# Two ordinary tiles instead of four ahead of the seven-product tiles of a feed-forward stage

## What is computed

```python
def rmsnorm(x, g):
    xf = x.astype(jnp.float32)
    y = xf * lax.rsqrt(jnp.mean(xf * xf, axis=-1, keepdims=True) + EPS)
    return (y * g.astype(jnp.float32)).astype(x.dtype)

def swiglu(h, wg, wu, wd):
    return (jax.nn.silu(h @ wg) * (h @ wu)) @ wd
...
        h = rmsnorm(x, ffn_norm_g[layer, 0])
        x = x + 0.5 * swiglu(h, ffn_w_gate[layer, 0], ffn_w_up[layer, 0], ffn_w_down[layer, 0])
```

## Time and profile before

| what | us |
|---|---|
| median of three runs | 2056.39 |
| the profiled execution, its own time | 2056.34 |
| its span, first to last instruction | 2054.5 |
| PE busy | 2029.2 |
| DVE busy | 1555.1 |
| ACT busy | 1018.3 |
| POOL busy | 298.7 |

### The profile page before, as it was taken

The page is one execution under the profiler, slowest core; times in us unless marked ns, Lnnn a source line. Parts: engine busy times, 40 slices in busy tenths (PEclk is TensorE's granted clock), DMA queues, the critical chain, the costliest instruction groups (busy, mean ns, idle before and its releaser), DMA issues.

```text
span 2054.5 us, 34513 instructions
## 1 busy us (share of the span) xinstructions
PE 2029.2 (99%) x13775; PEld 1771.9 (86%) x13775; DVE 1555.1 (76%) x2437; ACT 1018.3 (50%) x1597; POOL 298.7 (15%) x287
## 2 busy tenths in 40 slices
PE   8999999999999999999999999999999999999999
PEld 6899999788888788999998899999866688999998
DVE  6877776596778898877776787777679857877775
ACT  5544444453436445544445444444467745444444
POOL 0111110001000001111110111111046500111110
PEclk9999999999999999999999999999999999999999
DMA  5333334332153423333333333333750122333332
GB/s 157 103 106 101 101 103 108 94 86 82 50 146 93 95 74 100 103 108 99 102 94 110 94 95 103 113 93 88 144 101 8 42 62 82 113 103 94 106 90 72
DMA packets 325284, 196.06 MB, mean 95 GB/s; under 512 B 14891, under 2 KB 317110, under 8 KB 325126
## 3 DMA queue, kind: packets, MB, share of 16 engines
q1 hardware_dynamic: 322502, 184.21, 30.9%
q0 software_dynamic: 2624, 9.67, 3.0%
HBM read 191.07 MB, written 2.79 MB: 94 GB/s over the span
## 4 chain that ended last, share of the span: by engine, by line
PE 66%; DVE 4%; POOL 2%; issue 1%; ACT 1%; DVEq 0%; ACTq 0%; POOLq 0%
PE ps L2014 9%; PE ps L2016 9%; PE ps L2015 9%; PE ps L2078 4%; PE ps L2079 4%; PE ps L2080 4%; PE ps L1892 3%; PE ps L1894 3%; PE ps L1893 3%; PE ps L2586 1%; PE ps L2101 1%; PE ps L2099 1%; PE ps L2100 1%; PE ps L2557 1%; POOL index_scores L538 1%
## 5 line engine op out<-in xcount | busy, mean ns | idle before, releaser
L560 ACT ACTIVATE w_hi<-w_raw 128x1024 fp32r<-128x1024 f32 (+1 forms) x351 | 361.9, 1033 | 208.9 <-PE ps L1894 109.9
L1034 DVE TENSOR_TENSOR w_lo<-w_raw,w_hi 128x1024 fp32r<-128x1024 f32 (+1 forms) x351 | 419.9, 1196 | 43.5 <-ACT w_hi L560 43.2
L472 POOL TENSOR_TENSOR sq<-w_raw 128x512 f32<-128x512 f32 x72 | 96.6, 1341 | 1179.5 <-DMA w_raw<-in_ffn_w_up 1137.1
L2016 PE MATMUL ps<-h_hi,w_lo 128*128 128x256 f32 x864 | 244.5, 283 | 0.0
L2014 PE MATMUL ps<-h_hi,w_hi 128*128 128x256 f32 x864 | 244.2, 283 | 0.0
L2078 PE MATMUL ps<-act_hi,w_hi 128*128 128x512 f32 x512 | 200.0, 391 | 0.0
L2079 PE MATMUL ps<-act_lo,w_hi 128*128 128x512 f32 x512 | 200.0, 391 | 0.0
L2080 PE MATMUL ps<-act_hi,w_lo 128*128 128x512 f32 x512 | 199.2, 389 | 0.0
L2014 PEld LDWEIGHTS ps<-h_hi,w_hi 128*128 128x128 f32 x864 | 165.6, 192 | 2.7
L2016 PEld LDWEIGHTS ps<-h_hi,w_lo 128*128 128x128 f32 x864 | 165.6, 192 | 0.0
L614 ACT ACTIVATE silu_gate<-silu_gate 128x256 f32<-128x256 f32 x144 | 59.8, 415 | 212.9 <-DVE silu_gate L1228 209.8
(11 more groups left out here) (409 smaller groups left out, 5208.8 us busy)
## 6 DMA issues: line engine op xcount, KB each, us to landing
w_raw<-in_ffn_w_gate SPq DMA_DIRECT2D x88, 512.0 KB, 3.8
w_raw<-in_ffn_w_up SPq DMA_DIRECT2D x88, 512.0 KB, 3.8
w_raw<-in_ffn_w_down SPq DMA_DIRECT2D x64, 512.0 KB, 3.4
w_raw<-in_hy_w_in SPq DMA_DIRECT2D x44, 512.0 KB, 3.8
w_raw<-in_ffn_w_down SPq DMA_DIRECT2D x32, 384.0 KB, 3.5
w_raw<-in_hy_w_out SPq DMA_DIRECT2D x16, 512.0 KB, 4.0
acum_rows<-acum_scratch POOLq DMA_DIRECT2D x4, 1024.0 KB, 10.2
bias_rows<-line_scratch POOLq DMA_DIRECT2D x8, 512.0 KB, 11.4
```

What stands on the lines that cost most here:

```text
L560: act.activation(w_hi[:, s, 0:width[n]], w_raw[:, s, 0:width[n]], ACT.Copy).then_inc(hi_ready, 1)
L1034: dve.tensor_tensor(w_lo[:, s, 0:width[n]], w_raw[:, s, 0:width[n]], w_hi[:, s, 0:width[n]].bitcast(F32), ALU.subtract).then_inc(lo_ready, 1)
L2016: mm = pe.matmul(dst, wl, rh[:, k, :], start=False, stop=k == 3, skip_group_check=True)
```

## The change

The phases become 2, 4, 4, 4 and 8 tiles, and PLAIN becomes 2. So twenty tiles of a stage are seven-product tiles. Sixteen of them (2 to 17) have a pack behind them: the packs behind tiles 2 to 5 hold 12 matmuls (two tiles' worth), the other twelve 24. Tiles 18 to 21 have none. The eight final down outputs have 24 matmuls each. The openings of ScalarE, VectorE and TensorE are written anew, the product `a` of the first seven-product tile goes to bank 4, which its pack waits for, and the fourth input sum of the stages ffn1 to ffn3 gets a buffer of its own. The number of units, their order in the slots and the number of updates of x per stage stay.

```diff
-PHASES = ((0, 4), (4, 4), (8, 4), (12, 4), (16, 6))
-PLAIN = 4
+PHASES = ((0, 2), (2, 4), (6, 4), (10, 4), (14, 8))
+PLAIN = 2
...
+        s4_hi = at("s4_hi", [P, 4, TOK // 2], 92, F32R)
...
         def gate_unit(st, f):
-            return UB[st] + 2 * f + max(0, min(f, LAST + 4) - 4)
+            return UB[st] + 2 * f + max(0, min(f, LAST + 4) - PLAIN)
...
+        def packed(f):
+            return PLAIN <= f < LAST + 4
+
+        def pack_of(f):
+            f0, nf = PHASES[(f - PLAIN) // 4]
+            return f0, nf, (f - PLAIN) % 4
...
-            for m in range(KT):
-                width[gate_unit(st, FT - 1) + 2 + m] = LAST_N * P
+            for f in range(PLAIN, PLAIN + 4):
+                width[pack_unit(st, f)] = 2 * PHASES[0][1] * P
...
-                    if i == 3:
+                    if i == 3 and q == 0:
                         act.wait_ge(unit_used, n + 2 * PLAIN)
...
                 if st == STAGES[0]:
                     rms_out(st)
+                    produce_hi(n + 4)
                 for k in range(KT):
                     act.activation(s_raw[:, k, :], x[:, k, :], ACT.Copy, scale=gains[:, GAIN[st] + k:GAIN[st] + k + 1]).then_inc(s_hi_ready, 1)
-                produce_hi(n + 4)
+                if st != STAGES[0]:
+                    produce_hi(n + 4)
+                    rms_out(st)
+                    s_high(0)
+                silu(0)
                 if st == STAGES[0]:
-                    silu(0)
-                else:
-                    rms_out(st)
-                s_high(0)
+                    s_high(0)
                 s_high(1)
...
                 produce_hi(n + 5)
+                act_high(0)
+                t_high(PLAIN)
                 s_high(2)
...
                 if st == STAGES[0]:
                     line_out()
...
+                silu(1)
+                keep(PLAIN, 0)
+                s_high(3)
+                produce_hi(n + 6)
+                act_high(1)
+                keep(PLAIN, 1)
+                keep(PLAIN, 2)
+                produce_hi(n + 7)
+                keep(PLAIN, 3)
+                silu_half(PLAIN, 0)
+                t_high(PLAIN + 1)
+                produce_hi(n + 8)
+                for f in range(PLAIN + 1, FT):
                     nxt_unit = gate_unit(st, f) + 2
...
+                    silu_half(f - 1, 1)
                     produce_hi(nxt_unit)
...
+                    if not packed(f - 1):
                         keep(f, 0)
                     act_high(f - 1)
                     if f < FT - 1:
                         t_high(f + 1)
...
+                    if packed(f - 1):
                         keep(f, 0)
                     produce_hi(nxt_unit + 1)
...
+                    if packed(f):
                         produce_hi(nxt_unit + 2)
...
+                    keep(f, 1)
+                    silu_half(f, 0)
                     keep(f, 2)
                     keep(f, 3)
...
                 if st == STAGES[0]:
                     scaled(0)
+                    produce_lo(n + 4)
                 h_sums()
-                produce_lo(n + 4)
+                if st != STAGES[0]:
+                    produce_lo(n + 4)
+                    scaled(0)
                 s_low(0)
...
+                product(0)
                 s_low(1)
...
+                last_weight_sums(PLAIN)
                 produce_lo(n + 5)
+                act_low(0)
+                t_low(PLAIN)
+                scaled(1)
                 s_low(2)
...
+                product(1)
+                s_low(3)
+                last_weight_sums(PLAIN + 1)
+                act_low(1)
+                gate_low(PLAIN)
                 produce_lo(n + 6)
...
                 produce_lo(n + 7)
...
+                up_sums(PLAIN)
+                t_low(PLAIN + 1)
                 produce_lo(n + 8)
...
-                for f in range(PLAIN, FT):
+                for f in range(PLAIN + 1, FT):
...
-                    b, a, c = (ps[:, bank + j, HALF[0]] for bank in (BB, BA, BC))
+                    b, a, c = (ps[:, bank, HALF[0]] for bank in (BB + j, 4 if first else BA + j, BC + j))
...
+                    if f == PLAIN:
+                        pe.wait_ge(gate_low_steps, 2 * kb + 1)
...
-                for f in (2, 3):
-                    pe.wait_ge(gate_scaled, gb + f)
-                    unit(n + 2 * f, 2 * (f % 2), h_hi, h_lo, KT)
-                    pe.wait_ge(up_scaled, fb + f - 1)
-                    unit(n + 2 * f + 1, 2 * (f % 2) + 1, h_hi, h_lo, KT)
```

More of the change, by code:

```diff
@@ L686, in ffn @@
                         t_high(f + 1)
-                    if f != PLAIN and f - 1 != LAST + 4:
+                    if packed(f - 1):
                         keep(f, 0)
                     produce_hi(nxt_unit + 1)
[L690 to L693, removed]
+                    if packed(f):
                         produce_hi(nxt_unit + 2)
-                        keep(f, 1)
-                        silu_half(f, 0)
+                    keep(f, 1)
+                    silu_half(f, 0)
                     keep(f, 2)
@@ L1241, in ffn @@
                     scaled(0)
+                    produce_lo(n + 4)
                 h_sums()
-                produce_lo(n + 4)
+                if st != STAGES[0]:
+                    produce_lo(n + 4)
+                    scaled(0)
                 s_low(0)
-                if st != STAGES[0]:
-                    scaled(0)
+                product(0)
                 s_low(1)
-                product(0)
+                last_weight_sums(PLAIN)
                 produce_lo(n + 5)
+                act_low(0)
+                t_low(PLAIN)
+                scaled(1)
                 s_low(2)
-                act_low(0)
+                product(1)
[3 more added lines that the diff above has]
+                gate_low(PLAIN)
                 produce_lo(n + 6)
-                scaled(1)
-                last_weight_sums(PLAIN)
-                product(1)
                 produce_lo(n + 7)
-                act_low(1)
-                t_low(PLAIN)
+                up_sums(PLAIN)
+                t_low(PLAIN + 1)
                 produce_lo(n + 8)
-                scaled(2)
-                product(2)
-                produce_lo(n + 9)
-                act_low(2)
-                for f in range(PLAIN, FT):
-                    nxt_unit = gate_unit(st, f) + 2
-                    added = 4 <= f - 1 < LAST + 4
-                    if f == PLAIN:
-                        scaled(f - 1)
-                    else:
-                        gate_high(f - 1)
+                for f in range(PLAIN + 1, FT):
+                    nxt_unit = gate_unit(st, f) + 2
+                    gate_high(f - 1)
                     product(f - 1)
@@ L2020, in ffn @@
                 s1, s2, s3 = ((s_hi[:, i, :, :], s_lo[:, k0:k0 + 4, h]) for i, k0, h in ((1, 4, HALF[1]), (0, 0, HALF[0]), (2, 0, HALF[1])))
-                s4 = h_hi[:, 0:4, HALF[1]], s_lo[:, 4:8, HALF[0]]
+                s4 = s4_hi[:, :, :] if q else h_hi[:, 0:4, HALF[1]], s_lo[:, 4:8, HALF[0]]
                 def seven(f):
@@ L2037, in seven @@
                     product(b, gate, 0, *a11, True).then_inc(prod_done, 1)
-                    if first:
-                        pe.wait_ge(gate_scaled, gb + PLAIN + 1)
-                    elif second:
+                    if second:
                         pe.wait_ge(up_scaled, fb + PLAIN)
-                    else:
+                    elif not first:
                         pe.wait_ge(gate_low_steps, 2 * (k - 2) + 1)
@@ L2066, in down_pack @@
                 def down_pack(f):
-                    u, i, f0 = pack_unit(st, f), f % 4, f // 4 * 4 - 4
+                    u, (f0, nf, i) = pack_unit(st, f), pack_of(f)
                     s = u % SLOTS
                     pe.wait_ge(lo_ready, u + 1)
+                    if f == PLAIN:
+                        pe.wait_ge(gate_low_steps, 2 * kb + 1)
                     for j in range(2):
-                        pe.wait_ge(x_upd, XB[st] + 2 * (f - 4) + j - 1)
-                        for k in range(4):
+                        pe.wait_ge(x_upd, XB[st] + 2 * (f - PLAIN) + j - 1)
+                        for k in range(nf):
                             if i == 0:
@@ L2123, in ffn @@
                     seven(f)
-                    if f < LAST + 4:
+                    if packed(f):
                         down_pack(f)
```

49 lines of the change are left out of this document (13 added, 36 removed).

## The result

The changed kernel takes 2118.73 us (median of 4 runs, 2117.48 to 2120.55) against 2056.43 of the kernel before: 1.0304 times as long, 95% interval 1.0292 to 1.0317, or 62 us more. The profiled execution took 2117.66 us with a span of 2115.9. The time lies inside the range given, 14 us above the forecast.

The account below looks back on a forecast made before the run. The prediction took TensorE to bound the kernel: fewer matmuls save 6.8 us, but new waits in openings and ends, less old waits, make +49 in all, so 2056.3 + 49 = 2105 us, range 2080 to 2126.

Parts of the forecast that it names:

- What bounds the kernel: Whole kernel: TensorE, busy 2029.2 of 2054.5 us, sets the span, and every new wait of it lengthens the span.
- What the matmuls give, -6.8: Two ordinary tiles become seven-product tiles, 10.92 to 10.07 us each: 1.7 us a stage, 6.8 over four; down projection costed at nothing.
- The first wait: Third product of tile 2, waiting for VectorE's three `s_low`: 2.2 us in ffn2, 4.5 with mutual blocking; 11.3 in ffn0.
- GpSimd beside VectorE: Stage openings: GpSimd's weight sums and VectorE operations with two SBUF inputs block each other, 1.8 us for tile 2, 0.5 tile 3.
- The upper bound: Openings: every meeting of GpSimd's sums with such VectorE operations, `s_low` included, blocks as in rows 7; total +49 against +31 without.
- The second wait, 5.8: Third product of tile 3, behind tile 4's up unit load, weight sums, `t_high` and `keep`: 5.8 us, 4.1 without blocking.
- Tiles 4 to 6, and 19 and 20: Late `keep` evictions: 2.0 us a stage in tiles 4 to 6; 1.1 us at the fifth product of tiles 19 and 20 each.
- The sum: Whole kernel: +11.3 us each in ffn1 to ffn3, +15 in ffn0, together +49, or +31 without mutual blocking.
- a rival with a chance of 0.15: Clock falls in eight new waits of 4.5 us or more, costing 24 us more: 2129; chance 0.15 for above 2120.
- matmuls more than 0.12 us apart: Sign that would prove the forecast wrong: 256-column matmuls starting further apart than this, which would be the clock.
- Not slower: Rival: the openings keep up, with `s_low(2)` and tile 4's load early enough; 2042, or 2049.5 with old waits; chance 0.10.
- Only the ends wait: Rival: opening keeps up, but tiles 4 to 6 and 19, 20 lose 3 to 4 us a stage; 2050 to 2062; chance 0.07.

Follow-up runs that it names:

- e8: Changed kernel with GpSimd's weight sums of tiles 3 and 4 on 16 of 512 columns, the rest left out: 2102.97 us.
- e6: Changed kernel with unused-result matmuls ahead of the third product of tile 2 only (90 in ffn0, 34 in ffn1 to ffn3): 2118.87 us.
- e3: Changed kernel with ScalarE's keep(f, 1) ahead of the next up unit's high part in tiles whose predecessor has no pack: 2114.12 us.
- e5: Changed kernel with 34 unused-result matmuls per stage ahead of the third product of tile 3 only: 2112.00 us.
- e1: Changed kernel whose first seven-product tile waits for one input low part per product instead of three before the third: 2117.55 us.
- e12: Kernel before with e11's edit, plus ffn0's unit n+4: high part behind ScalarE's third copy, low part ahead of the input sums: 2053.75 us.
- e4: Changed kernel with units n+6 and n+7 split on ScalarE and VectorE ahead of the fourth input sum's split: 2116.64 us.
- e10: Changed kernel with e1, e3, e4, e5 and e9 together: 2105.18 us.
- e7: Changed kernel with VectorE's four input sums on 16 of 256 columns, the rest of that work left out: 2102.37 us.
- e11: Kernel before with keep(f, 1) of each stage's first seven-product tile ahead of the high parts of the next two units: 2054.11 us.
- e9: Changed kernel with ffn0's high part of unit n+4 behind the third of ScalarE's eight copies instead of ahead of them: 2116.81 us.

## Why the prediction was right, and by how much it missed

**What bounds the kernel.** Right: TensorE sets the span, and gaps and slow matmuls between its starts explain 60.4 of the 61.4 us by which it grew.

**What the matmuls give, -6.8.** Right as a count: undisturbed seven-product tiles take 10.07 us, and the final down outputs 43.55 for 192 matmuls, 0.227 each, as costed.

**The first wait.** Right to 0.1 us where its list holds. Moved by the 32.55 us between the two traces (tile 2 at 1178.51 for 1145.96), the forecast has the sums begin at 1166.33 and the third `s_lo` end at 1185.75; measured 1166.26 and 1185.64. (The steps as listed in the forecast add up to 16.9, not 17.1; they are rounded.) In ffn1 it is 5.96: there VectorE makes one low part of 1.22 us between the norm and the sums, so they begin 10.96 us ahead of tile 2, not 12.25, and the wait is longer by about as much. I had taken ffn2 for all three. ffn0 came at 11.24 for 11.3, closer than that wait repeats.

**GpSimd beside VectorE.** The upper bound, which I took, was right: `s_low(0)` and the product cost 0.72 + 1.09 = 1.8 us more, `s_low(2)` 0.5. The rule of the Trainium skill, SBUF — State Buffer, "Who interferes with whom", holds for the meeting that was open: two SBUF inputs on VectorE and a reading GpSimd block each other, and an `s_lo` of 1.21 us becomes 1.76 to 1.94. e8 confirms it: without most of GpSimd's work beside them, `s_lo` and the product take 1.22 and 0.69. What blocking costs in time was not tried by itself, as e8 takes away GpSimd's own time as well.

**The second wait, 5.8.** The chain was right link by link: issue at 1193.05 (forecast 1160.5, or 1193.05 moved), landing after 4.9 for 4.7, sums, `t_high` and `keep` with TensorE at 1204.64 (forecast 1204.45). What failed is the other end, "Tile 2 ends at 1160.5": moved, that is 1193.05, and it ended at 1194.54, as its products behind the first wait ran at 1.2 GHz. TensorE came 1.5 us later and so waited 4.48. e6, which keeps the clock up there, measured 5.6 to 5.9 in all four stages: the forecast's number.

**Tiles 4 to 6, and 19 and 20.** 2.0 a stage became 1.6, and 1.1 became 1.05. In tile 19 the mechanism was right: e3 takes the wait away by the order alone. In tile 20 the order is not all of it, since in e3 a meeting with GpSimd, which the forecast did not have there, keeps 0.86.

**The sum.** It was +49 and came out +62. The term that was mis-sized is the clock: I gave it to a rival with a chance of 0.15 and nothing in the sum. The rival had the fall right at every long wait, and its price wrong: 3 us for each of eight, 24, where slow matmuls make 15.4 and e5 gives back 6.7, all of it behind the second waits. Its counterargument, that work behind a wait is dense here, did not keep the clock. The prediction had named matmuls more than 0.12 us apart as a sign that it was wrong, and on this point it was. The rule of the Trainium skill, TensorE: Matmul & The Clock Gate, "Part 1: The HAM clock gate", that idle time brings the half clock as the default, agrees with all eight, though a wait of 3.02 us in e1 and one of 3.24 in e12 did not bring it. By the table's rows, the first waits are 1.4 us above the forecast, the second waits 5.7 below it, tiles 4 to 6 and 19 and 20 together 2 below, and the slow matmuls 15.4 above. That is +9 of the 12.4 between 49 and the 61.4 of the spans; the rest I have not settled. So the forecast came as close as it did partly by luck: the slow matmuls that it left out also shortened the second waits that it had put in at full length.

**The rivals on the other side.** *Not slower* asked for `s_low(2)` early and an earlier load. e4 sent the load 1.3 us earlier against its stage and gained about 2; e10, with every reordering I had, stays at +49. *Only the ends wait* fell: the ends are 8.4 of 51.8 us.

## What to carry to other kernels

Fixed work of other engines at the opening of a stage needs a stretch of the bounding engine that asks nothing new of them. Before trading such a stretch for fewer instructions, lay the other engines' lists against it: here 1.7 us of matmuls a stage were bought with half the cover, and the waits came to 13 us a stage. Price a new wait at both ends, when the input is ready and when it's asked for. Put the fall of the clock behind a long wait into the sum, but only where no later wait on another engine's list takes it up.

## What the runs showed of the hardware

- The clock does not go by the length of a wait alone. It stayed up over the wait of 2.1 us in the kernel before, over first waits of 0.9 to 1.9 us in e7, over 3.02 us in e1 (the window there) and over 3.24 us in e12 (granted clock 1.00 in the 13.8 us behind it). It fell behind the same wait of 2.1 us in e11 (0.65 in the 4.9 us behind it) and at second waits of 2.3 us in e8, whose timeline of TensorE and window right behind the wait read:

```profile
1196.87 0.35 PE L2014 MATMUL ps<-s_hi,mix_hi 128*128 128x256 f32 x1 [2.12 <-ACT silu_gate L633]
...
1196.87:1200.00 3.13, 3.13 (x18) 3.13 (x19) 3.10 (x5) 2.44 (x4) 0.00 (x0) 0.65 0.57 166
```

- TensorE is 100% busy in that window, and its granted clock is 0.65.
- Time that matmuls lose to the half clock is not all lost to the kernel: they lost 15.4 us, and keeping the clock up gave back 6.7 (e5).
- A meeting of GpSimd and VectorE costs both: 1.29 + 2.27 us on GpSimd for 2.6 alone, 1.94 + 1.78 on VectorE for 1.9. Moving an instruction earlier can make such a meeting where there was none, as in e9.
